# Re-ordering the steps around the third projection and the first top-k of a fused two-block kernel

## The reference

```
x = x + merged @ w_out                                  # third projection of the block: "wo2"
h = rmsnorm(x, norm_xa_g);  m = rmsnorm(mem, norm_mem_g)
x = x + softmax((h @ w_q) K^T / sqrt(128)) V @ w_o      # cross attention, 4 heads: "xq", then "xo"
h = rmsnorm(x, norm_ffn_g)
q = (h @ w_q)                                           # 8 heads x 2 halves x 128: "pq"
s = einsum("thpd,hpnd->thpn", q, subkeys)               # 128 keys for each half
s1, i1 = top_k(s[:, :, 0], 16);  s2, i2 = top_k(s[:, :, 1], 16)
cand   = s1[..., :, None] + s2[..., None, :]            # 256 candidates
top_s, pos = top_k(cand, 16);  e = (i1 * 128 + i2) at pos
g = softmax(top_s);  a = gelu(einsum("td,thkd->thk", h, w_down[e]))
y = einsum("thk,thkd->td", g * a, w_up[e])              # rows of two tables of 16384 x 1024
return rmsnorm(x + y, final_g)
```

## Time and profile before

| | us |
|---|---|
| median of 3 runs | 1361.63 |
| lowest, highest | 1359.74, 1363.78 |
| the profiled execution's own time | 1360.63 |
| its span in the trace | 1358.9 |
| PE busy | 1210.7 (89%) |
| DVE busy | 931.5 (69%) |
| ACT busy | 531.8 (39%) |
| POOL busy | 293.8 (22%) |
| chain that ended last, share of PE | 56% |
| share of the DMA of rows (R) in it | 30% |

### The profile page before, as it was taken

One profiled execution on the slowest core, in us unless ns is written; L12 is line 12 of the kernel. 1 busy time (PEld: TensorE's weight loads), 2 busy tenths in 40 slices (PEclk: granted clock), 3 DMA queues, 4 the chain that ended last, 5 costly groups with the idle time before them and its releaser, 6 DMA issues.

```text
span 1358.9 us, 17473 instructions
## 1 busy us (share of the span) xinstructions
PE 1210.7 (89%) x6452; PEld 884.5 (65%) x6452; DVE 931.5 (69%) x1824; ACT 531.8 (39%) x955; POOL 293.8 (22%) x261
## 2 busy tenths in 40 slices
PE   7999999999999999999988999998777777777775
PEld 7999998899988899998774554444332222323322
DVE  6765748866665575557587877767777776776655
ACT  4843236545543446645543332333222222222312
POOL 0000000000000000000024545455444445444430
PEclk9999999999999999999999999999999999999999
DMA  7543235545565644357669999999999999999994
GB/s 275 184 169 144 94 106 212 193 152 179 184 221 202 208 170 171 140 185 280 263 247 377 419 419 420 419 419 420 419 421 420 419 421 419 421 420 419 420 420 185
DMA packets 55788, 396.76 MB, mean 292 GB/s; under 512 B 6304, under 2 KB 6304, under 8 KB 8352
## 3 DMA queue, kind: packets, MB, share of 16 engines
q0 software_dynamic: 36864, 268.45, 47.8%
q1 hardware_dynamic: 17136, 119.42, 24.6%
q10 hardware_dynamic: 1712, 7.87, 1.6%
HBM read 394.67 MB, written 1.05 MB: 291 GB/s over the span
## 4 chain that ended last, share of the span: by engine, by line
PE 56%; DMA 30%; DVE 7%; ACT 5%; issue 2%; POOL 0%; DVEq 0%; ACTq 0%; SPq 0%; POOLq 0%
DMA R<-experts,IDX 30%; PE ps L540 25%; PE ps L1081 10%; PE ps L623 10%; PE ps L590 3%; PE ps L552 2%; DVE w_lo L1616 1%; DVE JUNK L2310 1%; ACT w_hi L1131 1%; PE ps L931 1%; PE ps L732 1%; PE ps L720 1%; ACT DIAG L1495 1%; PE ps L658 0%; DMA raw<-weights 0%
## 5 line engine op out<-in xcount | busy, mean ns | idle before, releaser
L1081 PE MATMUL ps<-R,DIAG 128*128 128x512 f32 x1020 | 479.9, 617 | 116.9 <-ACT DIAG L1495 114.5
L1081 PEld LDWEIGHTS ps<-R,DIAG 128*128 128x128 f32 x1020 | 189.2, 194 | 386.6 <-issue 197.1
L2471 POOL DMA_INDIRECT R<-experts,IDX x256 | 291.6, 1139 | 545.0 <-PE ps L1081 311.1
L2310 DVE CUSTOM_DVE_ANT_0 JUNK<-R,XN 128x1024 f32<-128x1024 f32 x256 | 313.7, 1225 | 135.1 <-DMA R<-experts,IDX 129.5
L1616 DVE TENSOR_TENSOR w_lo<-raw,w_hi 128x1024 fp32r<-128x1024 f32 x206 | 243.4, 1224 | 98.3 <-ACT w_hi L1131 94.9
L1131 ACT ACTIVATE w_hi<-raw 128x1024 fp32r<-128x1024 f32 x206 | 206.0, 1050 | 89.0 <-DMA raw<-weights 86.6
L540 PE MATMUL ps<-opC_lo,w_hi 128*128 128x256 f32 x544 | 155.4, 286 | 3.7 <-DVE opC_lo L1586 2.4
L540 PE MATMUL ps<-opC_hi,w_hi 128*128 128x256 f32 x544 | 154.7, 284 | 0.0
L540 PE MATMUL ps<-opC_hi,w_lo 128*128 128x256 f32 x544 | 154.6, 284 | 0.0
L1487 ACT ACTIVATE act_d<-dots,rst 128x2 f32<-128x2 f32 (+1 forms) x130 | 38.3, 295 | 271.4 <-DVE dots L2310 271.2
L1495 ACT ACTIVATE DIAG<-con,coef 128x128 f32<-128x128 f32 x255 | 88.6, 394 | 114.4 <-DVE coef L2320 110.6
(11 more groups left out here) (358 smaller groups left out, 1664.7 us busy)
## 6 DMA issues: line engine op xcount, KB each, us to landing
raw<-weights SPq DMA_DIRECT2D x104, 1024.0 KB, 4.9
PQW<-weights SPq DMA_DIRECT2D x6, 1024.0 KB, 9.2
R<-experts,IDX POOLq DMA_INDIRECT x256, 30.7
LNR<-rows ACTq DMA_DIRECT2D x3, 1024.0 KB, 7.7
XF<-xT SPq DMA_DIRECT2D x2, 512.0 KB, 6.0
raw<-weights SPq DMA_DIRECT2D x2, 512.0 KB, 6.5
MEM<-mem ACTq DMA_DIRECT2D x1, 1024.0 KB, 7.7
XR<-x ACTq DMA_DIRECT2D x1, 1024.0 KB, 5.2
```

What stands on the lines that cost most here:

```text
L1081: mm = pe.matmul(psum[:, 4 + 2 * m + n, :], DIAG[:, k, :], rows_[:, D + n * 512:D + (n + 1) * 512], start=(it % 8 == 0 and k == 0), stop=True,
L2310: dve.tensor_tensor_reduce(out=JUNK[:, :], in0=rows_[:, 0:D], in1=XN[:, it // 8, :], scale=1.0, scalar=0.0, op0=ALU.mult, op1=ALU.add, acc ...
L2471: pool.indirect_dma_start(out=R[u][:, :], out_offset=None, in_=experts, in_offset=bass.IndirectOffsetOnAxis(ap=IDX[:, it, k:k + 1], axis=0 ...
```

## The change

Three lists are re-ordered; no operation is added or taken away, except that one table switch moves.

- **h3 and ax.** The counters of the split parts are renamed, so that the low part of side 1, half 1 of the norm comes after the attention values of side 0 (`values_hi(0)` ahead of `hi_side(1, 1)`, `values_lo(0)` ahead of `lo_side(1, 1)`).
- **wo2.** The half (m 0, g 1) is added and squared ahead of (m 1, g 0), and the weight halves of `xq` go first.
- **xq to xo.** ACT runs `cross_rows(1)` ahead of two weight halves; `warm(ACT.Exp)` moves ahead of `rows_across("h4Ta", 0)`; `root_side(3, 0)` with its table of the square root follows `cross_exps` instead of going ahead of them.
- **First item.** PE: `sums(0, 0)` right behind `query(2, 0)`, `head_scores(2, 0)` and the two turns behind it, and then `sums(0, 1)`, half of `query(3, 0)`, `sums(0, 2)`, the other half. ACT: `activate(0, 0)` ahead of `head_scores(2, 0)` and the squares; `queries(3, 0)`, then `warm(ACT.Sqrt)`, `root_side(4, 1)` and `gate_exp(1)` behind `activate(0, 2)`. DVE: `dot_rows(0, 0)` first, `inverse_side(4, 1)` behind `coefs(0, 2)`.
- **Units.** The two opened units go to rows 14 and 22 instead of 10 and 19. Worked out from the table, n = 8 follows row 0, n = 9 to 13 follow rows 2 to 6, n = 14 waits for the query of head 0, side 1, n = 15 to 21 follow rows 7 to 13, n = 22 waits for the query of head 1, side 1, and n = 23 and 24 follow rows 14 and 15.

```diff
@@ OPENED
-        for n, u, j in ((10, 3, 0), (19, 0, 1), (35, 14, 2), (52, 15, 3), (69, 7, 4), (86, 4, 5), (99, 9, 6),
+        for n, u, j in ((14, 3, 0), (22, 0, 1), (35, 14, 2), (52, 15, 3), (69, 7, 4), (86, 4, 5), (99, 9, 6),
@@ PE
             query(2, 0)
-            head_scores(2, 0)
-            turn_side("h4Tb", 0, 1, 0, 7)
-            turn_side("h4Tb", 1, 1, 1, 8)
-            query(3, 0)
...
             sums(0, 0)
+            head_scores(2, 0)
+            turn_side("h4Tb", 0, 1, 0, 7)
+            turn_side("h4Tb", 1, 1, 1, 8)
+            sums(0, 1)
+            query(3, 0, (0,))
+            sums(0, 2)
+            query(3, 0, (1,))
             head_scores(3, 0)
+            sums(0, 3)
             query(0, 1)
-            sums(0, 1)
-            sums(0, 2)
+            sums(0, 4)
             head_scores(0, 1)
-            sums(0, 3)
             query(1, 1, (0,))
-            sums(0, 4)
+            sums(0, 5)
             query(1, 1, (1,))
-            sums(0, 5)
             sums(0, 6)
@@ ACT, wo2 to xo
             hi_side(0, 0)
-            square_side("wo2", 2, 1, 0)
             upper_half(xq + 1, 0)
-            square_side("wo2", 3, 0, 1)
             upper_half(xq + 1, 1)
+            square_side("wo2", 2, 0, 1)
             hi_side(0, 1)
             root_side(1, 0)
+            square_side("wo2", 3, 1, 0)
...
             upper_half(xo, 0)
+            values_hi(0)
+            hi_side(1, 1)
+            upper_half(xo, 1)
+            square_side("wo2", 4, 1, 1)
+            warm(ACT.Sqrt)
+            root_side(2, 1)
+            cross_rows(1)
+            upper_half(xo + 1, 0)
+            upper_half(xo + 1, 1)
             act.wait_ge(xn_gain, 4)
...
             square_side("xo", 1, 0, 0)
+            warm(ACT.Exp)
             rows_across("h4Ta", 0)
             square_side("xo", 2, 0, 1)
-            root_side(3, 0)
-            warm(ACT.Exp)
             cross_exps(1, 0)
             cross_exps(1, 1)
+            warm(ACT.Sqrt)
+            root_side(3, 0)
@@ ACT, first item
             gate_exp(0)
-            warm(ACT.Sqrt)
+            queries(2, 0)
+            activate(0, 0)
+            head_scores(2, 0)
             square_side("xo", 3, 1, 0)
             square_side("xo", 4, 1, 1)
+            activate(0, 1)
+            rows_across("h4Tb", 1)
+            activate(0, 2)
+            queries(3, 0)
+            warm(ACT.Sqrt)
             root_side(4, 1)
-            queries(2, 0)
-            head_scores(2, 0)
-            rows_across("h4Tb", 1)
-            activate(0, 0)
-            queries(3, 0)
-            activate(0, 1)
+            gate_exp(1)
             head_scores(3, 0)
+            activate(0, 3)
             queries(0, 1)
-            gate_exp(1)
-            activate(0, 2)
+            activate(0, 4)
             head_scores(0, 1)
-            activate(0, 3)
-            activate(0, 4)
             activate(0, 5)
@@ DVE, first item
             top_a(1)
             top_b(1)
+            dot_rows(0, 0)
             residual_side("xo", 3, 1, 0)
+            residual_side("xo", 4, 1, 1)
+            coefs(0, 0)
             gain_side(1, 1, 0)
-            residual_side("xo", 4, 1, 1)
             gain_side(1, 1, 1)
+            dot_rows(0, 1)
             mean_side(4, 1)
-            dot_rows(0, 0)
+            coefs(0, 1)
+            top_c(1)
+            top_d(1)
+            dot_rows(0, 2)
+            rows_across("h4Tb", 1)
+            coefs(0, 2)
             inverse_side(4, 1)
-            rows_across("h4Tb", 1)
-            top_c(1)
-            coefs(0, 0)
-            dot_rows(0, 1)
-            top_d(1)
-            coefs(0, 1)
-            dot_rows(0, 2)
             top_e_(1)
             top_f(1)
-            coefs(0, 2)
             dot_rows(0, 3)
             top_g(1)
+            coefs(0, 3)
             top_h(1)
-            coefs(0, 3)
             dot_rows(0, 4)
```

More of the change, by code:

```diff
@@ L82 @@
 for _n, _p in [("x", 2), ("pooled", 4), ("o", 4), ("m", 4), ("mem", 4), ("ln1", 4), ("h", 16),
-               ("h2", 4), ("at", 2), ("gm", 2), ("m2", 4), ("h3", 4), ("ax", 2), ("h4", 4)]:
+               ("h2", 4), ("at", 2), ("gm", 2), ("m2", 4), ("h3", 3), ("ax", 1), ("h3c", 1), ("axc", 1)]:
     SPLIT[_n] = _k
@@ L341, in build, with norm_parts, values_parts @@
         TURNED = ("ln1T", "h2T")
+        def norm_parts(m, q):
+            return ("h3c", 0) if m and q else ("h3", 2 * m + q)
+        def values_parts(m):
+            return ("ax", "axc")[m], 0
         def norm_turn(m, q):
@@ L981, in cross_query @@
                     w = take(b % 4, half_end(b, h))
-                    has_lo(pe, "h3", 2 * m + k)
+                    has_lo(pe, *norm_parts(m, k))
                     for i in (2 * h, 2 * h + 1):
@@ L1048, in _ @@
             cross_query(1, [(0, 1), (1, 0), (1, 1)])
-            has_lo(pe, "ax", 0)
+            has_lo(pe, *values_parts(0))
             side("xo", AXo, 0, 0)
@@ L1064, in _ @@
             head_scores(1, 0)
-            has_lo(pe, "ax", 1)
+            has_lo(pe, *values_parts(1))
             side("xo", AXo, 0, 1)
@@ L1453, in _ @@
                           ).then_inc(rows2_in, 16)
-            square_side("wo2", 4, 1, 1)
-            warm(ACT.Sqrt)
[L1456 to L1462, removed]
             cross_across(1)
             square_side("xo", 1, 0, 0)
+            warm(ACT.Exp)
             rows_across("h4Ta", 0)
             square_side("xo", 2, 0, 1)
-            root_side(3, 0)
-            warm(ACT.Exp)
             cross_exps(1, 0)
             cross_exps(1, 1)
+            warm(ACT.Sqrt)
+            root_side(3, 0)
             def head_scores(j, m):
@@ L1509, in _ @@
             gate_exp(0)
-            warm(ACT.Sqrt)
+            queries(2, 0)
+            activate(0, 0)
+            head_scores(2, 0)
             square_side("xo", 3, 1, 0)
             square_side("xo", 4, 1, 1)
-            root_side(4, 1)
-            queries(2, 0)
-            head_scores(2, 0)
-            rows_across("h4Tb", 1)
-            activate(0, 0)
-            queries(3, 0)
-            activate(0, 1)
+            activate(0, 1)
[3 more added lines that the diff above has]
+            warm(ACT.Sqrt)
+            root_side(4, 1)
+            gate_exp(1)
             head_scores(3, 0)
+            activate(0, 3)
             queries(0, 1)
-            gate_exp(1)
-            activate(0, 2)
+            activate(0, 4)
             head_scores(0, 1)
-            activate(0, 3)
-            activate(0, 4)
             activate(0, 5)
@@ L2122, in lo_side @@
             def lo_side(m, q):
-                j = 2 * m + q
                 pa = batch(dve, *norm_turn(m, q))
-                has_hi(dve, "h3", j)
+                has_hi(dve, *norm_parts(m, q))
                 sl = (slice(None), slice(4 * q, 4 * q + 4), slice(m * P, (m + 1) * P))
@@ L2153, in values_lo @@
                 pa = batch(dve, name)
-                has_hi(dve, "ax", m)
+                has_hi(dve, *values_parts(m))
                 ts = slice(m * P, (m + 1) * P)
@@ L2170, in _ @@
             low(xq, 1)
-            residual_side("wo2", 2, 1, 0)
-            residual_side("wo2", 3, 0, 1)
+            residual_side("wo2", 2, 0, 1)
             gain_side(0, 0, 1)
@@ L2177, in _ @@
             mean_side(1, 0)
+            residual_side("wo2", 3, 1, 0)
+            inverse_side(1, 0)
             gain_side(0, 1, 0)
-            inverse_side(1, 0)
             cross_max(0, 0)
@@ L2188, in _ @@
             low(xo, 0)
+            values_lo(0)
             lo_side(1, 1)
+            low(xo, 1)
             mean_side(2, 1)
-            values_lo(0)
             inverse_side(2, 1)
-            low(xo, 1)
             low(xo + 1, 0)
@@ L2199, in _ @@
             gain_side(1, 0, 1)
+            cross_max(1, 0)
             rows_across("h4Ta", 0)
-            mean_side(3, 0)
-            inverse_side(3, 0)
-            cross_max(1, 0)
             cross_max(1, 1)
@@ L2206, in _ @@
             cross_weights(1, 1)
+            mean_side(3, 0)
+            inverse_side(3, 0)
             def firsts(it):
```

## The result

The changed kernel takes 1375.38 us (median of 4 runs, 1374.47 to 1376.78) against 1361.31 us for the kernel before beside it: a ratio of 1.0104, 95% interval 1.0090 to 1.0119, or **14.1 us slower**. The forecast was 8.8 us slower, 1370.4 us; the measured time lies 1.4 us above its main range of 1365.8 to 1374 and inside its wider one, 1361 to 1377. The profiled execution after took 1376.09 us with a span of 1374.4; that of before had 1358.9, so the traces differ by 15.5 us, and these I take apart.

The account below looks back on a forecast made before the run. The stream of rows was taken to bound the kernel: its start, plus holes, plus a constant. -1.6 - 2.6 + 13.0 = +8.8 us gave 1369.4 for the profiled execution, 1370.4 for the median; range 1365.8 to 1374 (0.70), wider 1361 to 1377.

Parts of the forecast that it names:

- Part 1: Ahead of the first top-k: the re-ordered lists start the stream of rows earlier, -1.6 us (bounds 0 and -2.5).
- PE's first wait: PE's 1.12 us wait at 647.90 for a low part: weight halves and side (0, 1) first, 1.3 us earlier.
- the second: PE's 1.01 us wait at 665.85: attention values ahead of `h3c` gain some 0.5 us more.
- The switch ahead of the copy of the first query: ACT, `root_side(3, 0)` behind `cross_exps`: 1.53 us of table switch ahead of that copy, 682.0 instead of 681.82, +0.2 us.
- Part 2: First item, 715 to 720 us: earlier `sums(0, 0)` and `sums(0, 1)` bring row 9 in time; the old hole closes, -2.6 us.
- Part 3: First item: DVE waits 8.5 us at `inverse_side(4, 1)`, later rows come late; new holes 8.2 + 3.0 + 1.8 = +13.0 us.
- the first: Rival: DVE's wait ends before the queue is empty, so the stream never runs dry; 1357.4 us, chance 0.08.
- The smaller hole: Rival: n = 13 and n = 14 come 3 to 4 us earlier, new holes 6 us; 1363.4 us, chance 0.12.
- The stall didn't recur: Rival: in the next five items late pairs cost again, 4 to 8 us more; 1376 us, chance 0.10.
- the switch of tables ahead of the root: ACT, first hole: priced at 1.53 us; by the skill's figure of about 2.66 it would add 1.1 us.

Follow-up runs that it names:

- filled_half: The changed kernel with unread matmuls added on PE, 15 ahead of `sums(0, 0)` and 30 ahead of `sums(0, 3)`: 1371.72 us, ratio 1.0084 to the kernel before.
- sums_first: part1 with sums 1 to 3 ahead of `query(0, 1)`, ACT's list to match, opened units at rows 15 and 20: 1358.85 us, ratio 0.9985.
- part1: The kernel before with only the re-ordering around `wo2`, `xq` and `xo`, first item and opened units as before: 1359.78 us, ratio 0.9985.

## Why the prediction was right, and where its sizes were off

Direction and mechanism held; the sum of 8.8 was 5.3 us short of the medians and 6.7 of the traces.

**Part 1 held.** Forecast -1.6, measured -1.9 at the first issue. PE's first wait begins its matmul at 646.57 instead of 647.90, 1.3 earlier as estimated, the second another 0.4 (estimated 0.5). The switch ahead of the copy of the first query cost nothing of it: 679.99 for 681.82.

**Part 2 failed, by 3.1 us.** `sums(0, 0)` started at 702.52 (foretold 702.3). Then I charged them the 3.6 to 3.7 us of the earlier trace rows, a duration from a PE that had worked up to them, and the list gave them 4.00 us of idle time first: 6.30. `sums(0, 1)` began at 712.22 (709.6), n = 9 went at 714.48 (711.9), and the hole of 3.5 us stayed, 4.0. I had written that the closing would be lost from 4 us of lateness on; 2.6 sufficed. Besides, this term has no worth of its own. The sum takes 2.6 us for the closing and then measures the next hole from the earlier point at which the queue runs dry, so a closing that fails shortens the next hole by as much. What the late `sums(0, 0)` cost is that all behind them was late too, n = 13 included.

The traces bear this out. In after and the seven kernels that keep its opened units, n = 22 is issued at very different times, from 750.51 to 766.57, but from that issue to the end of the span it is always 611.8 to 614.1 us, whatever was lost ahead. The forecast had n = 22 at 757.6 and, by its sum (a span of 1367.7), the end 610.1 behind it; measured are 762.62 and 611.8. So 5.0 of the 6.7 us that the trace is over the sum are the lateness of this row, and 1.7 lie behind it.

**Part 3: the stall to the tenth, its consequences short by 5.** DVE's idle time was 8.47 us (8.5). `sums(0, 3)` came at 732.52 (730.0), late by the first sums alone, and took 6.66 instead of 3.6: n = 13 at 736.57 (732.3), n = 14 at 743.02 (737.8), n = 22 at 762.62 (757.6). The missed 2.6 and 3.0 us of clock are the 5 us. filled_half shows it: clock kept, each step is within 1 us of the forecast (n = 22 at 756.69). There was a second term. Even so its lost time was 16.5 us, against my 13.0, for two reasons. One is that I had the queue run dry too late. Nine rows are 9.44 MB, and by the windows of after (to 710, and 334 GB/s from 710 to 715) they are through at 715.0, where I had row 8 leave at 716.4. The other is that I counted a hole as over when packets flow. With one or two rows queued they don't fill the engines: from 745 to 770 the share is 0.95 in after, but the rate 352 GB/s.

**The clock could have been foreseen.** Had I read PE's long idle times in the trace of before, these stood there, near the end (sums of two pairs, then the window):

```profile
1300.58 8.83 PE L1081 MATMUL ps<-R,DIAG 128*128 128x512 f32 x16 [2.48 <-ACT DIAG L1495]
```
```profile
1302.00:1307.00 5.00, 5.00 (x9) 2.05 (x8) 2.63 (x5) 0.99 (x3) 2.48 (x2) 0.66 1.01 416
```

Two pairs at 3.70 are 7.4 us at most; these took 8.83. (The same trace also has the opposite, as the last section shows.) I read that 89% of PE's time is busy and that PE decides nothing behind 745, and didn't ask what my own forecast idle times of PE, 4 and 7 us, would do to the work behind them.

**Rivals.** The stream did run dry, against the first. The smaller hole fell, it was larger. The stall didn't recur: from 770 on 420 GB/s. That this rival's 1376 is nearest to the measured time is chance. And the switch of tables ahead of the root took 1.53 us again (724.33 to 725.86), so no part of the error is its. The Trainium skill (ScalarE: Activation LUTs, What ACT_TABLE_LOAD costs) would have it at about 2.66; the measurement decides.

## What to carry to other kernels

When a re-ordering leaves TensorE idle for some us, price the matmuls behind the idle time at the lower clock as well, not only at the row of a busy stretch, and look whether the next transfer hangs on them. When a queue must not run dry, ask of each engine's list what else stands behind the moved wait: taking one waiter away (the root) only uncovered the next (`activate(0, 3)`), and the gain came when all of the pair went ahead of it. And count the holes of a stream from the last dry point: where the queue runs dry again, a hole ahead of that point costs nothing by itself, and closing it gives nothing.

## What the runs showed of the hardware

In the first item the x8 of a pair (four float32 matmuls of 512 columns, two passes each) took 6.78 us behind 3.07 us of idle time, 6.56 behind 3.89, 6.30 behind 4.00 and 6.66 behind 7.44, and 3.70 behind 1.68 and 1.86; two pairs (x16) took 8.83 behind 2.48 (before, near the end) and 8.78 behind 3.15 (sums_first). So the price was 1.4 to 3.1 us at each such place, and it hardly grew with the idle time.

But the length of one idle time doesn't decide alone whether the clock falls. Two lines of before say so:

```profile
746.92 3.70 PE L1081 MATMUL ps<-R,DIAG 128*128 128x512 f32 x8 [3.15 <-ACT DIAG L1495]
...
1137.93 8.83 PE L1081 MATMUL ps<-R,DIAG 128*128 128x512 f32 x16 [1.93 <-ACT DIAG L1495]
```

The first ran at full clock behind 3.15 us of idle time. The second did not behind 1.93 (the granted clock is 0.81 from 1135 to 1140 us and 0.84 in the next 5). And where before took 8.83 us behind 2.48, near the end, part1 has 3.70 for x8 behind 2.49 at the same place (1298.41). What decides at such lengths stays open here; behind 3.2 us and more the sums of the first item were slow in every trace without a filling.

Unread matmuls in the idle time kept the granted clock at 1.00 (filled_half, 710 to 745 us), and with 13 of them the time was lower than without, though by no more than the intervals allow. A float32 matmul of 128 columns showed as two passes, 14.01 us for 124, so 0.23 us for each matmul. And the share of busy DMA engines overstates a shallow queue: 0.95 at 352 GB/s, where a full queue shows 1.01 at 420.
